# First pass of five tiles, then groups of four, with a down projection in seven half-size products

## The reference

```
h = rmsnorm(x) ;  a | u | v = h @ w_in                  # 1024 -> 512 | 512 | 512
d = trailing mean of a over 2/4/8/16 tokens - a         # four channel groups of 128
p = einsum('btgc,gce->btge', d, pool_w) * pool_scale    # 128 x 128 map per group
m = gelu(u) * (W_s gelu(v) + b)                         # per chunk of 128 tokens, four heads
x = x + concat(p, m) @ w_out                            # 1024 -> 1024
x = x + relu(rmsnorm(x) @ w_up)**2 @ w_down             # 1024 -> 4096 -> 1024
y = rmsnorm(x)
```

## Time and profile before

| | |
|---|---|
| median of 3 runs | 1327.34 us (1325.18 to 1345.45) |
| span of the profiled execution, slowest core | 1324.9 us, 2.4 below the median |
| spans of the eight cores | 1320.0 to 1324.9 us |
| PE, PEld busy | 1262.8 us (95%), 675.4 us (51%) |
| DVE, ACT, POOL busy | 542.9 us (41%), 445.2 us (34%), 51.2 us (4%) |
| moved by DMA | 228.40 MB, mean 172 GB/s |

### The profile page before, as it was taken

How to read it: one execution, slowest core, us unless ns; L and a number is a source line. 1 busy time by engine, 2 the same in 40 slices (tenths; PEclk the granted TensorE clock), 3 DMA queues, 4 the chain that set the end, 5 groups by cost and what they waited for, 6 DMA issues and landing times.

```text
span 1324.9 us, 19827 instructions; the slowest of 8 cores (1320.0 to 1324.9 us)
## 1 busy us (share of the span) xinstructions
PE 1262.8 (95%) x7136; PEld 675.4 (51%) x7136; DVE 542.9 (41%) x1147; ACT 445.2 (34%) x809; POOL 51.2 (4%) x96
## 2 busy tenths in 40 slices
PE   4778999999899999999999999999999999999995
PEld 2444554455454554555455455445545545554552
DVE  4553444535443543444244254325435433451312
ACT  4434231224432432443152333235224323430411
POOL 4000000001000000000000000000000000000000
PEclk9788999999999999999999999999999999999998
DMA  9992887555725743653564474356357345645751
GB/s 175 202 230 84 151 198 145 149 154 169 244 67 196 246 154 132 212 172 133 203 204 160 159 230 155 143 199 196 128 191 251 135 151 200 119 159 193 259 200 48
DMA packets 39921, 228.40 MB, mean 172 GB/s; under 512 B 6848, under 2 KB 7104, under 8 KB 17040
## 3 DMA queue, kind: packets, MB, share of 16 engines
q1 hardware_dynamic: 26528, 172.49, 38.1%
q0 software_dynamic: 13296, 54.63, 18.6%
HBM read 215.05 MB, written 34.43 MB: 188 GB/s over the span
## 4 chain that ended last, share of the span: by engine, by line
PE 90%; DMA 5%; DVE 2%; ACT 2%; issue 1%; POOL 0%; DVEq 0%; ACTq 0%; POOLq 0%; SPq 0%
PE ps L658 28%; PE ps L640 26%; PE ps L530 9%; PE ps L373 8%; PE ps L602 6%; PE ps L622 6%; PE ps L399 4%; DMA WV<-w_v 2%; PE ps L315 2%; DMA X<-xall 1%; DMA yall<-X 1%; PE ps L472 0%; DVE HB L304 0%; PE ps L486 0%; DVE X L681 0%
## 5 line engine op out<-in xcount | busy, mean ns | idle before, releaser
L640 PE MATMUL ps<-H2T,RING 128*128 128x384 bf16 x2304 | 390.2, 326 | 2.5 <-ACT ST L644 2.0
L658 PE MATMUL ps<-RING,ST 128*128 128x512 bf16 x1728 | 375.7, 379 | 0.0
L640 PEld LDWEIGHTS ps<-H2T,RING 128*128 128x128 bf16 x2304 | 223.7, 98 | 149.5 <-issue 3.3
L658 PEld LDWEIGHTS ps<-RING,ST 128*128 128x128 bf16 x1728 | 168.7, 98 | 201.1
L276 ACT ACTIVATE JUNK<-X 128x1024 bf16<-128x1024 f32 x100 | 105.6, 1056 | 353.1 <-DVE SSf L273 156.3
L644 ACT ACTIVATE ST<-ps 128x384 bf16<-128x384 f32 x288 | 136.3, 493 | 179.2 <-PE ps L640 178.0
L646 DVE TENSOR_TENSOR ST<-ST 128x384 bf16<-128x384 bf16 x288 | 96.0, 355 | 167.6 <-ACT ST L644 167.5
L373 PE MATMUL ps<-HT,WAU 128*128 128x384 bf16 (+1 forms) x704 | 121.5, 335 | 3.4 <-ACT HT L319 3.4
L663 DVE TENSOR_TENSOR X<-ps,X 128x512 f32<-128x512 f32 x54 | 37.3, 691 | 210.6 <-PE ps L658 210.6
L530 PE MATMUL ps<-WOUT,MIXT 128*128 128x512 bf16 x528 | 115.8, 379 | 0.9 <-DVE MIXT L505 0.9
L373 PEld LDWEIGHTS ps<-HT,WAU 128*128 128x128 bf16 x704 | 70.3, 100 | 52.6 <-issue 9.3
(11 more groups left out here) (78 smaller groups left out, 707.9 us busy)
## 6 DMA issues: line engine op xcount, KB each, us to landing
RING<-scr SPq DMA_DIRECT2D x144, 1024.0 KB, 6.0
RING<-w_mlp POOLq DMA_DIRECT2D x16, 1024.0 KB, 14.8
scr<-RING SPq DMA_DIRECT2D x16, 1024.0 KB, 12.0
X<-xall POOLq DMA_DIRECT2D x30, 512.0 KB, 7.5
yall<-X POOLq DMA_DIRECT2D x30, 512.0 KB, 7.7
WAU<-w_au POOLq DMA_DIRECT2D x4, 512.0 KB, 16.2
WOUT<-w_out POOLq DMA_DIRECT2D x2, 1024.0 KB, 29.1
X<-xall SPq DMA_DIRECT2D x3, 512.0 KB, 5.6
```

What stands on the lines that cost most here:

```text
L640: i_ = e.matmul(bank(ub)[:, 0:TOK], lhsT=RING[s][:, k, (m % 4) * 128:(m % 4 + 1) * 128], rhs=H2T[:, k, :], start=(k == 0), stop=(k == 7))
L658: i_ = e.matmul(bank(n)[:, :], lhsT=ST[:, kg * 8 + kk, n * 128:(n + 1) * 128], rhs=RING[s][:, kk, :], start=(kg == 0 and kk == 0), stop=(k ...
```

## The change

- Tiles are grouped as 3, 2, and seven times 4 (`GROUPS`). The first pass works on groups 0 and 1 (five tiles) together; all later groups have 512 tokens as moving columns. X becomes one tile of nine slots, filled in turn.
- The down projection of the seven groups of four is one 2 x 2 block product in Strassen's form: the hidden tile is split by tokens (256 and 256) and by depth (2048 and 2048), the weight by depth and by output half. Seven products of sums of blocks take the place of eight (`DN`, in the order 3, 4, 5, 7, 2, 1, 6). Sums of hidden blocks are made by VectorE (`ssum`, 1024 elements a partition each, partly in place), sums of weight blocks once, in the first pass (`wsum`, ten of them, 4096 elements a partition each), and stored to scratch. `POST` says to which blocks of X a product is added or from which it is taken; products 7 and 6 run on in the banks of 4 and 1.
- The pool map is multiplied into the first half of `w_out` once (`fold`), so `MIXT`'s pool part is the difference `d` itself. `w_out` no longer stays in SBUF: its halves stream through the ring twice 1 MiB a group.
- The inverse root of the norms is two POOL operations (`rs`, with `pow`) on its queue, where the casting DMAs, X loads and y stores also stand.
- The order is a list of steps (32 of `UP`, 28 of `DN`, each 8 matmuls) with side work laid behind step k (`side(k, ...)`).

```
+GROUPS = [(0, 3), (3, 2)] + [(5 + 4 * s, 4) for s in range(7)]
...
+            def ring_load(at):
...
+                if key[0] == "raw":
+                    q = key[1]
+                    add("pool", lambda e: e.dma_start(out=RING[s][:], in_=w_mlp[q]), writes=[("RING", s)], dma=f"ringc{s}")
+                    dst = ("up", q) if q < 8 else ("dn", 2, q - 8) if q in (8, 9) else ("dn", 5, q - 14) if q in (14, 15) else None
+                    if dst is not None:
+                        scr_store(dst, RING[s][:], [("RING", s)], f"scrst{s}")
+                else:
+                    src = key[:-1]
+                    add("sp", lambda e: e.dma_start(out=RING[s][:], in_=SCR[src]),
+                        reads=[("SCR", src)], writes=[("RING", s)], dma=f"ring{s}")
...
+            def rs(kind, j0, j1, np_=128):
...
+                add("pool", lambda e: e.tensor_scalar(out=S, in0=S, scalar1=EPS, scalar2=None, op0=ALU.add), writes=wr("SS"))
+                add("pool", lambda e: e.tensor_tensor(out=R, in0=S, in1=MHALF[0:np_, 0:j1 - j0], op=ALU.pow),
+                    reads=wr("SS") + ["MHALF"], writes=wr("RS"))
...
+            def fold(hh):
+                W, wr = (T0, T0R) if hh == 0 else (T1, T1R)
+                for g in range(4):
+                    fb = next_front()
+                    add("pe", lambda e, g=g, fb=fb: e.matmul(bank(fb)[:, :], lhsT=PWT[:, g, :], rhs=W[:, g, :], start=True, stop=True),
+                        reads=["GFB"] + wr, writes=[("BANK", fb)])
+                    add("act", lambda e, g=g, fb=fb: e.activation(out=W[:, g, :], in_=bank(fb)[:, :], func=AF.Copy),
+                        writes=[("BANK", fb)] + wr)
+                scr_store(("wo", hh), W, wr, f"scrstw{hh}")
...
+            def wsum(M, c, qa, qb, op, dst):
...
+                add("dve", lambda e: e.tensor_tensor(out=o[:], in0=RING[sa][:], in1=RING[sb_][:], op=op),
+                    reads=[("RING", sa), ("RING", sb_)], writes=wr)
+                scr_store(("dn", M, c), o[:], wr, ch)
...
+            def ssum(a, b, op, dst, j):
+                (aa, ar), (ba, br) = qblk(*a, j), qblk(*b, j)
+                oa, orr = (SB[:, j * 4:j * 4 + 4, :], [("SB", j)]) if dst == "SB" else (aa, ar)
+                add("dve", lambda e: e.tensor_tensor(out=oa, in0=aa, in1=ba, op=op), reads=ar + br, writes=orr)
+
+            OPER = {1: (0, 0), 2: "SB", 3: (0, 0), 4: (1, 1), 5: "SB", 6: (1, 0), 7: (0, 1)}
+            POST = {3: [(0, 1, ALU.add), (1, 1, ALU.add)], 4: [(1, 0, ALU.add)], 5: [(0, 0, ALU.subtract), (0, 1, ALU.add)],
+                    7: [(0, 0, ALU.add)], 2: [(1, 0, ALU.add), (1, 1, ALU.subtract)], 1: [(0, 0, ALU.add)],
+                    6: [(1, 1, ALU.add)]}
+            CONT = {7: 4, 6: 1}
...
+            def DN(i, M, c, n):
...
+                    for kk in range(8):
+                        i_ = e.matmul(bank(ub)[:, :], lhsT=lh(kk), rhs=RING[s][:, kk, :],
+                                      start=(c == 0 and kk == 0 and M not in CONT), stop=(c == 1 and kk == 7),
+                                      skip_group_check=(M in CONT))
...
+                if n == 1:
+                    ring_done(key)
+                if c == 1:
+                    for (rb, hh, op_) in POST[M]:
+                        x = xap(i, rb * 2 + n, hh * 512, (hh + 1) * 512)
+                        add("dve", lambda e, x=x, op_=op_: e.tensor_tensor(out=x, in0=x, in1=bank(ub)[:, :], op=op_),
+                            writes=[("BANK", ub), xres(i, rb * 2 + n)])
```

The first pass goes through the depth in two halves c: the up pieces of it, its four down pieces, and the five weight sums made from these, each followed by its store and by the next load into that buffer:

```
+                q11, q21, q12, q22 = 8 + c, 10 + c, 12 + c, 14 + c
+                side(nup + 2, L(wsum, 6, c, q11, q12, ALU.add, 0))
+                side(nup + 4, L(wsum, 7, c, q21, q22, ALU.add, 1))
+                side(nup + 9, L(wsum, 4, c, q21, q11, ALU.subtract, None), L(ring_done, ("raw", q21)))
+                side(nup + 11, L(wsum, 1, c, q11, q22, ALU.add, None), L(ring_done, ("raw", q11)))
+                side(nup + 14, L(wsum, 3, c, q12, q22, ALU.subtract, None), L(ring_done, ("raw", q12)))
+                side(nup + 19, L(ring_done, ("raw", q22)))
```

And the side work of a group of four (steps 0 to 31 are `UP`, 32 to 59 `DN`), j being the next group:

```
+                for t in range(4):
+                    side(16 + 4 * t + 3, L(ssum, (0, 0), (0, 1), ALU.add, "SB", t))
+                    side(32 + t, L(ssum, (0, 1), (1, 1), ALU.subtract, None, t))
+                    side(43 + t // 2, L(ssum, (1, 0), (1, 1), ALU.add, "SB", t))
+                    side(46 + t // 2, L(ssum, (1, 0), (0, 0), ALU.subtract, None, t))
+                    side(48 + t // 2, L(ssum, (0, 0), (1, 1), ALU.add, None, t))
+                if j < NG:
+                    for n in range(4):
+                        side(6, L(load_x, j, n))
+                        side(17 + n, L(N1_sq, j, n))
+                        side(21 + n, L(N1_apply, j, n))
+                        side(23 + n, L(N1_T, j, n))
+                    side(18, L(rs, "1", 0, 2))
+                    side(20, L(rs, "1", 2, 4))
+                    for m in range(8):
+                        side(27 + m, L(WI_au, j, m))
+                    for n in range(4):
+                        side(35 + n, L(WI_v, j, n))
...
+                    for g in range(4):
+                        side(31 + g, L(PL, j, g))
+                        side(39 + g, L(gate, j, g))
...
+                    for hh in range(2):
+                        for n in range(4):
+                            side(43 + hh * 4 + n, L(WO, j, n, hh))
+                    for n in range(4):
+                        side(48 + n, L(N2_sq, j, n))
+                        side(53 + n, L(N2_apply, j, n))
+                        side(55 + n, L(N2_T, j, n))
```

More of the change, by code:

```diff
@@ L213, in next_hb @@
[L213 to L223, removed]
@@ L230, in build_nc @@
[L230 to L240, removed]
@@ new lines, in PL_post, with gate, mm @@
+            def PL_post(i):
+                if i < LAST:
+                    T = ntok(i)
+                    add("dve", lambda e: e.tensor_copy(out=A[:, :, 0:16], in_=A[:, :, T:T + 16]),
+                        reads=[("A", g) for g in range(4)], writes=[("Ah", g) for g in range(4)])
+            def gate(i, g):
+                fb = next_front()
+                nt = GROUPS[i][1]
+                T = ntok(i)
+                def mm(e):
+                    for n in range(nt):
+                        wm = WSMTS if (i == LAST and n == 3) else WSMT
@@ new lines, in schedule @@
+            add("pool", lambda e: e.dma_start(out=IDB[:], in_=ident[:, :]), writes=["IDB"], dma="su0")
+            for m in range(0, 8, 2):
+                add("pool", lambda e, m=m: e.dma_start(out=WAU[:, m:m + 2], in_=w_au[:, m:m + 2]),
+                    reads=[("X", 0)] if m == 0 else [], writes=[("WAU", m), ("WAU", m + 1)], dma=f"wau{m}")
+            for n in range(2):
+                N1_sq(0, n)
+            rs("1", 0, 2)
+            N1_sq(0, 2)
+            sq("1", 3, XH, [("X", 8)], 16)
@@ new lines, in schedule @@
+            for n in range(2):
+                N1_sq(1, n)
+            rs("1", 0, 2)
+            for g in range(4):
+                PL(0, g)
+            PL_post(0)
+            for n in range(2):
+                N1_apply(1, n)
+            for n in range(3):
+                WI_v(0, n)
+            for n in range(2):
+                N1_T(1, n)
+            for m in range(4):
+                WI_au(1, m)
+            for g in range(4):
+                gate(0, g)
+            for m in range(4, 8):
+                WI_au(1, m)
@@ new lines, in schedule @@
+            add("sp", lambda e: e.dma_start(out=HSA[:], in_=hist[:, :, :, :]), writes=["HSA"], dma="hs")
+            for n in range(3):
+                for hh in range(2):
+                    WO(0, n, hh)
+                N2_sq(0, n)
+            rs("2", 0, 3)
+            for g in range(4):
+                gate(1, g)
+            for n in range(3):
+                N2_apply(0, n)
+            for n in range(4):
+                load_x(2, n)
+            for n in range(3):
+                N2_T(0, n)
```

1014 lines of the change are left out of this document (483 added, 531 removed).

## The result

The changed kernel takes 1290.01 us (median of 4 runs, 1289.96 to 1290.02). Its ratio to the kernel before is 0.9726, 95% interval 0.9709 to 0.9743: 2.7% less, where 5.1% and 1259 us were forecast. The span profiled is 1288.2 us on the slowest of eight cores (1284.0 to 1288.2). So it is faster, but by 36 us and not 68. Its time lies 0.01 us above the range, and 15 us above the 1245 to 1275 of the forecast's own case.

The account below looks back on a forecast made before the run. TensorE was taken as full, each removed steady-stage matmul a full gain: 88 front + 185.5 main part + 10 waits + 959.5 later groups + 4 seams + 10 tail = 1257, forecast 1259 us, range 1245 to 1290.

Parts of the forecast that it names:

- the forecast's own case: Whole kernel: the summed forecast holds, 1245 to 1275 us; chance 0.68.
- the count of 142.7 us a group: Steady group of four: 640 matmuls of 512 columns 138.2 us, 64 transposes 3.6, 16 gates 0.9; 35.67 per tile.
- group 2's waits: Group 2, first after the first pass: 8.4 us of waits for X behind y before, 0 after the change.
- Seams: Seams of seven groups of four: 4 us in the sum, up to 1.5 a group in the forecast's range.
- The front: Start until the first pass's main part: 88 us against 91.86 before, with 10 added for the fold's serial links.
- The main part: First pass after the front: 185.5 us of work plus 10 of wait, 5 at its start and 5 for raw-weight stores and loads.
- The tail: After the last matmul, which touches half a tile: norm steps and last store, 10 us against 13.5 before.
- First-pass chain: First pass: six links of raw loads and sum stores take 80 us, not 53; 24 more, 1283; chance 0.13.
- VectorE late: Product stage: block sums at 1.22 us and queued additions make products wait 4 us a group; +28, 1287; chance 0.08.
- Weight loads not covered: First pass: 256-column matmuls do not hide weight loads, 320 x 0.098 = +31 us, 1290; chance 0.02.
- a cheaper matmul of 512: Down projection: a 512-column matmul costs less than its row, products save 29 us and not 48, 1278; chance 0.01.
- Ring starved: Weight ring: 24 loads a group at 6.6 us each cost 15.7 a group, 110 in all, 1369; chance 0.08.

Follow-up runs that it names:

- gates_early: Changed kernel with the next group's four gates issued two a step (steps 39, 40) instead of one (39 to 42); ratio 0.9663 to the kernel before.
- best: Changed kernel with group 2's norm later, gates two a step, fold halves alternating, up-piece load reordered, final norm earlier, last tile's first half before tile 2; 1266.34 us.

## Why the prediction was wrong

The direction and the mechanism held. TensorE's matmuls bound the kernel before, a removed one was a gain in full, and the pace per matmul, the count of 142.7 us a group (142.78 once the gates' wait is gone), the 256-column price and the VectorE prices came out as summed. (VectorE's load of a stage was added up wrongly: 62 and 22 make 84 and not 80. It measured 73.6 and decided nothing.) The narrow matmuls, 6.98/64 = 0.109 us each (timeline of TensorE, first pass; the next instruction starts at 122.31):

```profile
115.33 7.15 PE L538 MATMUL ps<-ST,RING 128*128 128x256 bf16 x64 [1.27 <-ACT ST L343]
122.31 1.46 PE L538 MATMUL ps<-H2T,RING 128*128 128x384 bf16 x8
```

**The step that failed** is the one that put group 2's waits at nothing: "Now X is asked for at step 6, needed at step 17, 19 us later: 0." It measured 15.6, half of the 31.2 that were missing. On the slowest core 10.1 of it are waits for X and for the ring, 1.3 the gate's and some 3 low clock; on the others the waits for X, the ring or both are 7.5 to 10.4. The sum had taken nothing for either. Three things were wrong in it. X is not asked for at step 6: step 6 is only a place in POOL's queue, behind y stores that go out as the final norm of five tiles ends, and behind the landing of each y; the X loads went out 21.5 to 33.5 us into the stage. The landings were not asked about at all: 7.5 us for X before, 16 by the median of the changed kernel, and in group 2, where ring slots, five y, four X and the last weight sum meet, 17 for y as well. And the kernel before had lost 8.4 us in that very place. The prediction read all 8.4 as waits for X behind y, but its trace has 4.8 of waits behind an X (2.0 for ACT, 1.5 at the transposes, 1.3 for their copy), 1.4 of others and a granted clock of 0.97 over 54 us, with y landing after 22.1. The change put 15.2 MB where there had been 12.7 (54 us each), which no step of the sum asked about. I had reckoned the DMA engines by their mean over a stage (0.60, measured 0.59) and looked for trouble in the product stage, where the weights are used fastest; the trouble was where the queues start together.

*Seams* were 4 us and measured 9.9 (the range had allowed up to 1.5 a group). Most of it is one repeated wait, 6.8 us in groups 3 to 7: 1.3 us as the output projection waits for the last gate, which is behind additions to X on VectorE, in each stage from group 2 on that has a front in it, six in all (group 2's is in its own line of the table). Another 1.9 are two waits at the transposes. The gate's wait in the three stages from 739 to 1172 us:

```profile
PE ps L504 <- DVE HT L491: 4.2, 3, 1.6
```

I counted VectorE's load (46 of 77 us) and not the order at that step; gates_early takes the gate's wait away whole.

*The front* measured 4.3 over: the fold cost 9.7 (10 had been taken), and most of the rest is low clock. The input matmuls of group 1 took 9.6 and not 7.0 (granted clock 0.76 from 40 to 50 us, 0.90 from 50 to 60), its v 4.7 and not 3.5 (0.66 from 60 to 70, after the gaps of the fold). *The main part* took 13.2 us over its matmuls against 10, but not where they were put: 5 had been for the raw-weight chain, which cost nothing. It has 9.8 us of waits, and a granted clock of 0.98, which makes about 4 more (0.02 x 198.7, an estimate). The wait of 3.2 stands where VectorE is busy for 14.21 of 16 us (200 to 216 us), for the most part with group 2's trailing sums, for which the prediction had no price. These are its waits in full:

```profile
PE ps L339 <- DVE HB L330: 3.9, 5, 1.3
PE ps L475 <- DVE HT L491: 3.2, 1, 3.2
PE ps L538 <- ACT H2T L343: 1.4, 1, 1.4
PE ps L538 <- ACT ST L343: 1.3, 1, 1.3
```

*The tail:* 12.2 against 10; 1.1 of it is a POOL step of 0.23 that took 1.32 (below), the rest was not taken apart.

**The rivals.** *First-pass chain:* rejected, no wait of the main part is for a raw weight. *VectorE late:* the products never waited for a block sum (the L624 groups above have 0.0 of idle before them), but its relative, the gate behind additions, cost 1.3 a group, not 4. *Weight loads not covered* and *a cheaper matmul of 512*: rejected by 0.109 and 0.2158. The rule that the prediction quotes from the Trainium skill (TensorE: Matmul & The Clock Gate, Back-to-back issue gap: about 131 ns for 512 columns, 81 for 128) does not hold here in either kernel. *Ring starved:* no wait for RING on any core once group 2 is over; the page has 5.3 us to landing for product weights, below the 5.95 from which it would decide. But starved is what the ring was for one moment, in group 2 (2.2 to 9.2 us by core). That the time came out only 0.01 us above the range is luck: its upper end had room for these rivals, and none of them came about. The range was too narrow at its upper end because the crowding of a hand-over between stages stood in none of the cases.

## What to carry to other kernels

A DMA's time to landing is not a price of that DMA: it comes from what else is asked for in the same stretch, so look for the places where queues start together (a pass ends, buffers come free, outputs and the next inputs meet) and add up the bytes of that stretch, not of the stage. A wait found there before the change is the first place to reckon again, and a cure by order in such a stretch must give time to every user at once, or the wait moves to the next. A long landing by itself is no loss: in the best kernel X took 24 us to land and TensorE waited 3.1 us. Where the sum of matmuls fits the pace exactly, the rest of the time is a short list of waits that can be priced one by one.

## What was not expected of the hardware

At the end of the changed kernel a POOL step on one element a partition took 1.32 us beside a VectorE step of 1.28 whose two inputs lie in SBUF, and ended 0.09 us after it (timeline of the tail):

```profile
1278.50 1.28 DVE L649 SCALAR_TENSOR_TENSOR XS<-XS,RSf,GFB 128x1024 f32<-128x1024 f32 x1 [1.67 <-ACT JUNK L316]
1278.55 1.32 POOL L323 TENSOR_SCALAR SSf<-SSf 128x1 f32<-128x1 f32 x1 [0.29 <-ACT JUNK L316]
...
1280.02 0.56 POOL L324 TENSOR_TENSOR RSf<-SSf,MHALF 128x1 f32<-128x1 f32 x1
```

With the order of best the same step ran beside no VectorE operation and took 0.22:

```profile
1256.32 0.22 POOL L323 TENSOR_SCALAR SSf<-SSf 128x1 f32<-128x1 f32 x1 [0.29 <-ACT JUNK L316]
```

The Trainium skill has a rule for this: SBUF — State Buffer, section SBUF: two separate sides, has VectorE and GpSimd share a pair of ports that one of them holds for a whole instruction when a VectorE operation with two SBUF inputs meets a GpSimd one that reads SBUF. The two rows agree with it; no run here varied that alone. A second such meeting stands at the start of the changed kernel: from 12.2 to 16.7 us three POOL steps on one column took 1.2 to 1.4 us each beside VectorE's norm of the first tiles.
